# Norms by token block, roots on ScalarE and earlier turns on the way into attention

## The reference

```python
def rms_norm(x, g):
    y = x32 * lax.rsqrt(jnp.mean(x32 * x32, axis=-1, keepdims=True) + EPS)
# each sub-layer: h = rms_norm(x) * (1 + scale) + shift;  x = x + gate * block(h)
def mla_query(h, wdq, q_norm_g, wuq, q_qk_g):
    cq = rms_norm(h @ wdq, q_norm_g)                 # 512 wide: the query latent
    q = (cq @ wuq).reshape(b, s, N_HEADS, QK_HEAD_DIM)
    return rms_norm(q, q_qk_g)                       # then rotary on the last 64 of 192
def mla_compress(h, wdkv, kv_norm_g):
    kv_a = h @ wdkv                                  # 256 + 64 wide: the key latent
    return rms_norm(kv_a[..., :KV_LORA_RANK], kv_norm_g), kv_a[..., KV_LORA_RANK:]
def swiglu(t, w1, w3, w2):
    return (jax.nn.silu(t @ w1) * (t @ w3)) @ w2
```

## Time and profile before

| | us |
|---|---|
| median of 3 runs (lowest, highest) | 1496.22 (1495.68, 1496.23) |
| the profiled execution | 1492.56 |
| its span | 1490.8 |
| TensorE busy | 1384.3 (93%) |
| VectorE busy | 1074.7 (72%) |
| ScalarE busy | 745.6 (50%) |
| chain that ended last | PE 79%, DVE 12%, ACT 4%, issue 3%, DMA 2% |

### The profile page before, as it was taken

How to read it: one execution, slowest core, us unless ns; L and a number is a source line. 1 busy time by engine, 2 the same in 40 slices (tenths; PEclk the granted TensorE clock), 3 DMA queues, 4 the chain that set the end, 5 groups by cost and what they waited for, 6 DMA issues and landing times.

```text
span 1490.8 us, 18726 instructions
## 1 busy us (share of the span) xinstructions
PE 1384.3 (93%) x6689; PEld 1115.5 (75%) x6689; DVE 1074.7 (72%) x1384; ACT 745.6 (50%) x745; POOL 60.3 (4%) x97
## 2 busy tenths in 40 slices
PE   4999959999999979799999987999999999999986
PEld 1885427899999968577887767878787888878874
DVE  1687985534342456788888886889889888888886
ACT  2420243422222334465655533767777777777771
POOL 2000000400000000100000002000000000000001
PEclk9999969999999998799999997999999999999997
DMA  9898174994334232321222313999999999999983
GB/s 356 309 339 317 68 269 151 371 406 141 116 121 132 92 106 60 121 64 64 81 74 84 102 40 119 337 339 370 352 402 375 364 385 374 367 366 397 373 331 129
DMA packets 91017, 349.01 MB, mean 234 GB/s; under 512 B 6895, under 2 KB 43063, under 8 KB 61783
## 3 DMA queue, kind: packets, MB, share of 16 engines
q1 hardware_dynamic: 80672, 315.38, 57.2%
q0 software_dynamic: 8144, 26.52, 4.9%
q10 hardware_dynamic: 2151, 6.46, 1.1%
HBM read 324.01 MB, written 24.31 MB: 234 GB/s over the span
## 4 chain that ended last, share of the span: by engine, by line
PE 79%; DVE 12%; ACT 4%; issue 3%; DMA 2%; ACTq 0%; DVEq 0%; SPq 0%
PE ps L270 23%; PE ps L272 22%; PE ps L271 22%; DVE v L948 3%; PE ps L1754 2%; DVE wl L254 2%; ACT wh L248 2%; DVE hm L1382 2%; PE ps L1480 2%; PE ps L1785 1%; PE ps L1526 1%; PE ps L1758 1%; DMA raw<-in_conv_pw 1%; PE ps L329 1%; PE ps L1900 1%
## 5 line engine op out<-in xcount | busy, mean ns | idle before, releaser
L254 DVE TENSOR_TENSOR wl<-raw,wh 128x2048 fp32r<-128x2048 f32 x253 | 576.2, 2288 | 154.6 <-ACT wh L248 154.5
L248 ACT ACTIVATE wh<-raw 128x2048 fp32r<-128x2048 f32 x253 | 484.9, 1917 | 325.7 <-PE ps L272 279.4
L270 PE MATMUL ps<-wh,xgh 128*128 128x512 f32 x432 | 174.2, 403 | 0.0
L271 PE MATMUL ps<-wl,xgh 128*128 128x512 f32 x432 | 171.8, 398 | 0.0
L272 PE MATMUL ps<-wh,xgl 128*128 128x512 f32 x432 | 171.8, 398 | 0.0
L270 PE MATMUL ps<-hTh,wh 128*128 128x384 f32 x480 | 164.3, 342 | 0.0
L271 PE MATMUL ps<-hTl,wh 128*128 128x384 f32 x480 | 163.0, 340 | 0.0
L272 PE MATMUL ps<-hTh,wl 128*128 128x384 f32 x480 | 162.9, 339 | 0.0
L270 PE MATMUL ps<-wh,hgh 128*128 128x512 f32 x288 | 116.8, 406 | 7.6 <-DVE hgl L1388 4.1
L271 PE MATMUL ps<-wl,hgh 128*128 128x512 f32 x288 | 114.9, 399 | 0.0
L272 PE MATMUL ps<-wh,hgl 128*128 128x512 f32 x288 | 114.7, 398 | 0.0
(11 more groups left out here) (308 smaller groups left out, 2118.2 us busy)
## 6 DMA issues: line engine op xcount, KB each, us to landing
raw<-in_moe_w SPq DMA_DIRECT2D x180, 1024.0 KB, 6.1
raw<-in_ada_w SPq DMA_DIRECT2D x48, 1024.0 KB, 6.7
raw<-in_ffn_w SPq DMA_DIRECT2D x33, 1024.0 KB, 6.4
raw<-in_conv_pw SPq DMA_DIRECT2D x12, 1024.0 KB, 11.9
raw<-in_mla_wo SPq DMA_DIRECT2D x8, 1024.0 KB, 4.8
xs_dram<-hf POOLq DMA_DIRECT2D x14, 512.0 KB, 18.2
ys_dram<-hf POOLq DMA_DIRECT2D x14, 512.0 KB, 19.2
raw<-in_mla_wuq SPq DMA_DIRECT2D x8, 768.0 KB, 4.7
```

The lines of the kernel that those rows point to most:

```text
L248: act.activation(wh[:, split_no(s) % HL, :], raw[:, s % RAW, :], ACT.Copy).then_inc(hi_made, 1)
L254: eng.tensor_tensor(wl[:, split_no(s) % HL, :], raw[:, s % RAW, :], wh[:, split_no(s) % HL, :], ALU.subtract).then_inc(lo_made, 1)
L270: nc.tensor.matmul(out_, sh, mh, start=start, stop=False)
L271: nc.tensor.matmul(out_, sh, ml, start=False, stop=False)
```

## The change

Four things change.

1. **Norms "ffn" and "mla" by token block, roots on ScalarE.** ScalarE takes the square root of each block's sum itself (`Sqrt`, one column), VectorE only a reciprocal, each per block, as soon as that block's `x` is done. Block 0 is scaled by ScalarE, block 1 by VectorE, block 2 half by each. TensorE turns blocks 0 and 1 first and block 2 when it is there. A one-element `Sqrt` on a constant ahead of it brings the table in. The two ada chunks behind the "ffn" turns move into the first SwiGLU products (after k = 3 and k = 5).
2. **The SwiGLU's end.** The last product is computed block by block, so that blocks 0 and 1 are whole before block 2 begins; VectorE makes one `wl` chunk less ahead of the residual (it moves behind the fourth split block); on ScalarE `make_hi(MLA+2)` moves from behind the squares to behind the scaling of block 2.
3. **Latents.** The query latent's second half goes by token block; the key latent is turned after its second block; squares, roots and scalings go by block with `Sqrt` on ScalarE. `turn_cq` comes one key block earlier, and `queries(0)` runs k outermost and waits for each split block apart.
4. **First pair.** The turns use separate banks (3, 4 and 5, 7), so they no longer wait for one another's copies; the squares for the query norm move from ScalarE (out of `ps`) to VectorE (out of `q_sb`); GpSimd's clearing of `yacc` now also waits for `q_scaled`.

The core of the diff:

```diff
+        def norm_act_rows(act, q, layer, n, before_, banks, between=None):
+            act.activation(st[:, 63:64], epsc[:, 0:1], ACT.Sqrt)
+            for c in range(TC):
+                act.wait_ge(sem(before_), c + 1)
+                act.activation(xn[:, c, :], x[:, c, :], ACT.Square, scale=D ** -0.5,
+                               accum_out=st[:, c:c + 1]).then_inc(sem("squares"), 1)
+                act.wait_ge(*of_norm(q, "squares", TC, c + 1))
+                act.activation(st[:, 20 + c:21 + c], st[:, c:c + 1], ACT.Sqrt, bias=epsc[:, 0:1]).then_inc(sem("rooted"), 1)
+                if c == 1:
+                    act.wait_ge(sem("rstd"), RSTD[q] + 1)
+                    act.activation(xn[:, 0, :], x[:, 0, :], ACT.Copy, scale=st[:, 4:5]).then_inc(sem("normed"), 1)
+            act.wait_ge(sem("rstd"), RSTD[q] + TC)
+            act.activation(xn[:, 2, 512:D], x[:, 2, 512:D], ACT.Copy, scale=st[:, 6:7]).then_inc(sem("normed"), 1)
+            if between:
+                between()
...
+        def norm_dve_rows(dve, step, q, y, ready):
+            def inverse(c):
+                dve.wait_ge(sem("rooted"), ROOTED.index(q) * TC + c + 1)
+                dve.reciprocal(st[:, 4 + c:5 + c], st[:, 20 + c:21 + c]).then_inc(sem("rstd"), 1)
+                dve.wait_ge(sem("rstd"), RSTD[q] + c + 1)
+            for c in range(TC):
+                if c == 2:
+                    inverse(0)
+                ready(c)
+                step(dve.tensor_tensor(xn[:, c, :], y(c), gate[:, 1 if c == 0 else 0, :], ALU.mult))
+                dve.tensor_tensor(x[:, c, :], x[:, c, :], xn[:, c, :], ALU.add).then_inc(...)
+            inverse(1)
+            dve.tensor_scalar(xn[:, 1, :], x[:, 1, :], st[:, 5:6], None, ALU.mult).then_inc(sem("normed"), 1)
+            inverse(2)
+            dve.tensor_scalar(xn[:, 2, 0:512], x[:, 2, 0:512], st[:, 6:7], None, ALU.mult).then_inc(sem("normed"), 1)
+        def norm_pe_rows(pe, q, banks):
+            pe.wait_ge(sem("normed"), NORMED[q] + 2)
+            for j in range(4):
+                for c in range(2):
+                    pe.transpose(ps[:, banks[j], c * P:(c + 1) * P], xn[:, c, j * P:(j + 1) * P], ident[:, :])
+            pe.wait_ge(sem("normed"), NORMED[q] + 4)
+            for j in range(4):
+                pe.transpose(ps[:, banks[j], 2 * P:3 * P], xn[:, 2, j * P:(j + 1) * P], ident[:, :]).then_inc(sem("turned"), 1)
...
@@ ScalarE, query latent @@
-            act.wait_ge(chunk_used, MLA + 4)
+            query_latent(0)
+            query_latent(1)
+            for k in range(2):
+                act.wait_ge(sem("ck_turned"), k + 1)
+                act.activation(ckTh[:, k, :], ps[:, 3 + k, :], ACT.Copy).then_inc(sem("ck_hi"), 1)
+            query_latent(2)
@@ ScalarE, first pair @@
-            query_squares(0, turns())
             query_copy(0, turns())
...
@@ GpSimd @@
+            pool.wait_ge(sem("q_scaled"), 1)
             pool.memset(yacc[:, :, :], 0.0).then_inc(sem("yacc_zero"), 1)
@@ VectorE, SwiGLU's end @@
-            for i in range(2):
-                make_lo(dve, MLA + i)
+            make_lo(dve, MLA)
@@ VectorE, query latent @@
-            rsqrt(step, st[:, 6:9], st[:, 0:3], TC)
+            scale_cq(0)
+            scale_cq(1)
+            make_lo(dve, GRP + 1)
+            scale_cq(2)
@@ VectorE, first pair @@
-            query_sums(0, turns())
+            dve.tensor_tensor(pr[...], q_sb[...], q_sb[...], ALU.mult).then_inc(sem("q_square"), 1)
+            dve.wait_ge(sem("q_square"), 1)
+            dve.tensor_reduce(st[:, 32:38], pr[...], AX, ALU.add).then_inc(sem("q_summed"), 1)
@@ TensorE @@
-            norm_pe(pe, "ffn", FFN_BANKS, range(4))
-            for k in range(6, DK):
-                ada(GATE2 + k, 1, 2 * DK + k)
+            norm_pe_rows(pe, "ffn", FFN_BANKS)
...
+                if i == 1 and k in (3, 5):
+                    ada(GATE2 + (k + 9) // 2, 1, 2 * DK + (k + 9) // 2)
...
+            def ffn_down_last(s, mades):
+                wait_parts(pe, s)
+                for c, sub in ((0, 0), (1, 0), (0, 1), (1, 1), (2, 0), (2, 1)):
+                    pe.wait_ge(sem("ffn_lo"), mades[sub])
+                    last = ffn_down_part(s, sub, c, final=sub == 1)
...
```

More of the change, by code:

```diff
@@ L289, in hybrid_conv_mla_diffusion_step @@
         SPLITS = ("conv", "ln", "ffn", "mla")
+        NORMED = {"conv": 0, "ffn": TC, "mla": 2 * TC + 1, "moe": 3 * TC + 2}
+        RSTD = {"conv": 0, "ffn": 1, "mla": 1 + TC, "moe": 1 + 2 * TC}
         def of_norm(q, name, per, value):
@@ L349, in split_block @@
             dve.tensor_tensor(hTl[:, j, :], hf[:, j, :], hTh[:, j, :], ALU.subtract).then_inc(sem(q + "_h_lo"), 1)
-        def residual(dve, step, q, y, ready=None):
-            for c in range(TC):
-                if ready:
-                    ready(c)
-                step(dve.tensor_tensor(xn[:, c, :], y(c), gate[:, 1 if c == 0 else 0, :], ALU.mult))
-                dve.tensor_tensor(x[:, c, :], x[:, c, :], xn[:, c, :], ALU.add).then_inc(sem(q + "_x"), 1)
-            dve.wait_ge(sem(q + "_x"), TC)
         def kv_chunk(n):
@@ L707, in _ @@
             act.wait_ge(sem("tables_blank"), 32 * NT)
-            norm_act(act, "mla", 1, 0, "ffn_x", 0, MLA_BANKS, between=lambda: make_hi(act, MLA + 2))
+            norm_act_rows(act, "mla", 1, 0, "ffn_x", MLA_BANKS, between=lambda: make_hi(act, MLA + 2))
             act.wait_ge(chunk_used, MLA + 2)
@@ L1059, in _ @@
             dve.wait_ge(sem("gate_in"), 64)
-            residual(dve, step, "ffn", lambda c: ps[:, 2 * c:2 * c + 2, :].rearrange("p a b -> p (a b)"),
-                     lambda c: dve.wait_ge(sem("ffn_out"), c + 1))
-            norm_dve(dve, step, "mla")
-            split_dve(dve, "mla", "mla_modulated", 2)
+            norm_dve_rows(dve, step, "mla", lambda c: ps[:, 2 * c:2 * c + 2, :].rearrange("p a b -> p (a b)"),
+                          lambda c: dve.wait_ge(sem("ffn_out"), c + 1))
+            for j in range(DK):
+                split_block(dve, "mla", "mla_modulated", 2, j)
+                if j == 3:
+                    make_lo(dve, MLA + 1)
             for i in range(2, 4):
@@ L1091, in _ @@
             gained(tk, RD, KC)
-            dve.wait_ge(sem("ckv_squares"), TC)
-            rsqrt(step, st[:, 9:12], st[:, 3:6], TC)
+            dve.wait_ge(sem("rooted"), 2 * TC + 1)
+            step(dve.reciprocal(st[:, 9:12], st[:, 23:26]))
             for c in range(TC):
@@ L1106, in _ @@
             make_lo(dve, GRP)
-            make_lo(dve, GRP + 1)
-            dve.wait_ge(chunk_used, MLA + 4)
-            dve.tensor_tensor(kr_rot[:, :, :], kr0, kr1, ALU.add).then_inc(sem("kr_ready"), 1)
             for k in range(2):
@@ L1813, in _ @@
             turn_k(0, turns())
-            turn_r(0, turns())
-            turn_q(0, turns())
+            for c in range(KC):
+                last = pe.transpose(ps[:, 3, c * P:(c + 1) * P], krh[:, c, :, :].rearrange("p a b -> p (a b)"), ident[:, :])
+            last.then_inc(sem("first_turned"), 1)
+            pe.wait_ge(sem("q_copied"), 1)
+            for h in range(2):
+                for c in range(TC):
+                    last = pe.transpose(ps[:, 4 + h, c * P:(c + 1) * P], q_sb[:, 2 * c + h, 0:P], ident[:, :])
+            last.then_inc(sem("q_turned"), 1)
+            pe.wait_ge(sem("kT_made"), 1)
+            pe.wait_ge(sem("q_rotated"), 1)
+            for c in range(TC):
+                last = pe.transpose(ps[:, 7, c * P:(c + 1) * P], qr[:, 0, 2 * c:2 * c + 2, :].rearrange("p a b -> p (a b)"), ident[:, :])
+            last.then_inc(sem("r_turned"), 1)
+            pe.wait_ge(sem("rT_made"), 2)
             scores(0, turns(), False)
```

146 lines of the change are left out of this document (92 added, 54 removed).

## The result

| | before | changed |
|---|---|---|
| median, same chip (us) | 1496.22 | 1471.58 (1471.38 to 1472.04) |
| profiled execution, its span | 1492.56, 1490.8 | 1471.38, 1469.6 |
| mean granted TensorE clock | 0.964 | 0.975 |
| TensorE busy | 1384.3 (93%) | 1370.1 (93%) |

The changed kernel run again on another chip came to 1475.54 against 1494.50, ratio 0.9878 (0.9862 to 0.9895), 18.3 us. So some 6 us of the 24.6 are not there each time, and the first question is which. Small differences of medians are to be read with care: the executions of the kernel before on one chip lay between 1492.67 and 1495.75 us (19 of them), at mean granted clocks from 0.959 to 0.964, and each measurement has one trace.

What follows compares the result with a forecast made beforehand. TensorE bounds the stages; at the crossings small VectorE and ScalarE instructions do. Terms 3.7 + 3.0 + 2.5 + 2.0 + 3.4 = 14.6, less 0.7 and 0.4, give 13.5: median 1482.7 us, range 1479.0 to 1487.2.

Steps and rivals of the forecast that it cites:

- cold keys: First pair: TensorE idles up to 3 us ahead of `keys(1)` and may start it cold; 0.7 us lost.
- handovers: Across the sum: some eight handovers between engines, counted at nothing in the terms, at 0.05 each; 0.4 us off.
- way into attention: SwiGLU's end to the latents' first product: 3.95 us earlier, less 0.95 for longer low clock; 3.0 us, bounds 1.2 to 5.0.
- way into the SwiGLU: "ffn" norm to `turn_rows`: turns directly behind ada, 1.50 idle gone, new idle 1.7; 3.7 us gained, bounds 1.5 to 4.3.
- Rival C: First pair and latents: the clock stays high, 16.5 us gained, median 1479.7; chance 0.13.
- keys' end: Latents: key products end at 600.9 for 606.5, 2.5 us more gained, with a new wait of 1.3 ahead of `turn_cq`.
- queries': Latents: query products end at 607.4 for 614.9, the 1.96 idle gone; 2.0 us gained.
- from there to the second pair: First pair: maxima at 621.6 for 631.73, `pT` of pair 0 made 10.9 earlier, of which this stage gives 3.4 us.
- Rivals B: First pair: GpSimd or VectorE later than counted, memset not beside `wl` chunks or rotary tables late; 1485.4; chance 0.08.
- D: Pair loop: VectorE enters behind TensorE and every pair pays, 17 us lost, median 1499; chance 0.02.
- E: Most of the gain lost in an unseen wait, such as table loads around each root; 1494 to 1496; chance 0.04.
- Rival A: TensorE's clock takes more: cold products at the "ffn" start, first latent block, queries; about 4 us less gain, 1486.7; chance 0.10.

Runs made afterwards that it cites:

- two_moves: Changed kernel with ScalarE's `wh` chunk after the fourth modulated block, and VectorE's third query-latent scaling and turned-key sum before its `wl` chunk; 1480.25 us, ratio 0.9912.
- undo_memset: Changed kernel with GpSimd's memset of `yacc` freed from its wait for `q_scaled`; 1477.13 us.
- undo_first_pair: Changed kernel with the first pair as before: turns through banks 6 and 7, squares on ScalarE, `yacc` cleared without waiting for `q_scaled`; 1476.94 us, ratio 0.9893.

## Why the prediction was wrong

- **The step that failed is what was taken off the sum for TensorE's cold starts, and what the sum left out.** The steps as reckoned came to 15.55: the 0.95 for a longer cold start at attention is already off in 14.6 (3.95 less 0.95 is the term of 3.0), and 0.7 for cold keys and 0.4 for handovers went after it. Next to nothing of the 2.05 was paid. Behind the first product of the latents the clock was low for 2.9 us (to 558.46) in the changed kernel and 2.7 in before, where I had taken 4.6: 0.1 us and not 0.95. So the new stop ahead of it, 2.33 us in the trace, was not paid for in the low clock, in part or in full. The keys of pair 1 started at full clock (0.49 for their first product). The handovers can't be told one by one; the terms together lie above their sum without them.
- **From 15.55 to the 16.3 of the trace** it is sizes of single steps, about: VectorE was done with `krh` 8.7 us earlier, counted since the way into attention, for the 7.5 of the forecast (0.8 of the 1.2 is the unpaid cold start), and it took 13.0 from there to the maxima for 13.5; the way into the SwiGLU gave 0.3 less. From 13.5 to 16.3 that is 2.8 of the 11.1 missed.
- **Rival C had the number and not the cause.** The clock was high through the latents and the first pair, as it says, and its 16.5 is near to the 16.3; but the maxima hung on VectorE, and did so with the scores at 1.00 in the changed kernel and partly at 0.61 and 0.54 in `two_moves`. The match is luck.
- **The sum held everything outside its stretches still.** Routing moved by 3.6 with the phase of the clock, the pairs by 0.5, the convolution stage by 1.2, and the experts by -0.3. Of these the convolution's is no effect of the change: the changed kernel itself differed by 1.8 there in its second trace. It is no chance of one execution either, since the four executions of the first measurement lie within 0.7 us of each other and 3.4 below the lowest of the second. The routing's came in both pairs of traces, so it goes with these two kernels as they stand, but it is nothing that the changed lines do in that stage: 2.5 us of delay makes it 6.9 longer beside the delay.
- **The median.** 3.4 us are before's: I took a gain that was reckoned against 1492.56 off 1496.22. On four other occasions its median was 1493.37 to 1496.62. Even without these 3.4 us the time would lie below the range, as it does with the 18.3 us of the second measurement.
- By terms, first trace: way into the SwiGLU 3.4 for 3.7 (the new idle 2.09 for 1.7; the first product at 262.46, which is 263.6 on before's scale, for 263.1); the first residual at 541.88, which is 543.0 on before's scale, for 542.7; way into attention 3.8 for 3.0, the allowance that was hardly paid; keys' end 3.0 for 2.5 and queries' 2.1 for 2.0, with the new wait of 1.19 for 1.3; from there to the second pair 4.0, for 3.4 less the 0.7.
- The signs that I named came: no idle at L1558, `wh` ahead of L341, VectorE without idle from `krh` to the maxima, no table load between roots and copies, pairs of 34.00 us. The sign against me, "PEclk lower in the three stretches", did not; it was higher in all.
- Rivals B, D and E are out: the memset ran under the chunks, the loop's pairs kept their length, the loads stood once per group. Rival A did not come in the two traces of the changed kernel, but its first piece, cold products behind the gap on the way into the SwiGLU, came in `undo_memset` and cost 1.4 us; the sum had nothing for it, only the lower bound of its term.

What stays open: which phase a change will meet can't be read from the trace of before, and no run here made the routing stage short on purpose. Two measurements of the changed kernel, 0.9833 and 0.9878, have intervals that do not meet; their traces differ by 1.8 up to the convolution's residual and 2.2 in the experts, both at places of low clock, and whether that is the chip or the occasion was not tried.

## What to carry to other kernels

Where short waits chop TensorE's work, reckon each wait removed at the clock that the work behind it ran at, but only where TensorE sets the time, and take nothing off for cold work that no row shows: here 2.05 us of such allowances were next to nothing in the trace. Before a change of 1% is believed or dropped, compare the untouched stages in both traces; a stage of narrow products behind a wait is worth several microseconds either way with no line of it changed. A delay or a filler of known length ahead of that stage, put into both kernels, helps to tell such a shift from an effect of the code; it changes the wait as well as the start, so compare the two kernels with the same one.

## What the runs showed of the hardware that I had not expected

- TensorE can be busy and stay at the low clock: in `two_moves` 19.43 of 20.00 us busy with 128x8 products and 128-column turns, PEclk 0.50 throughout; with 30 products of 128x512 ahead of it, the clock was 1.00 at first and fell in the same work.
- GpSimd's memset holds up a small TENSOR_SCALAR (128x8) only for what is left of it: 1.54 us when the step met it early, 1.06 and 0.81 when later, 0.17 without (`before`, `undo_first_pair`, `undo_memset`, changed).
- A load of ScalarE's table took 1.28 us and hid wholly in its wait, since it stands ahead of the wait in the order; one root of one column took 0.29 with its bias.
